# Second attention: the masked corner and the rotary half swap move from TensorE to VectorE

## The reference, cut to what matters

```
def apply_rope(t, cos, sin):
    t1, t2 = jnp.split(tf, 2, axis=-1)
    return jnp.concatenate([t1 * cos - t2 * sin, t1 * sin + t2 * cos], axis=-1)

def mla_attention(q_nope, q_rope, k_nope, k_rope, v):       # 16 heads, 256 positions
    kchunk = jnp.arange(s_len) // CHUNK                      # CHUNK = 64
    ...
        s = (einsum(qn, k_nope) + einsum(qr, k_rope)) * scale      # 128 + 64 wide
        s = jnp.where(kchunk[None, :] <= qchunk[:, None], s, NEG_INF)
        prob = jax.nn.softmax(s, axis=-1)
        return einsum(prob, v)
```

## Time and profile before

| | |
|---|---|
| median of three runs | 2194.48 us |
| the profiled execution's own time | 2193.41 us |
| its span, first to last instruction | 2191.6 us |
| granted TensorE clock | 0.999 |
| PE busy | 2173.5 us (99%) |
| DVE busy | 1385.0 us (63%) |
| ACT busy | 1167.2 us (53%) |
| MLA layer | about 620 to 880 us |

### The profile page before, as it was taken

How to read it: one execution, slowest core, us unless ns; L and a number is a source line. 1 busy time by engine, 2 the same in 40 slices (tenths; PEclk the granted TensorE clock), 3 DMA queues, 4 the chain that set the end, 5 groups by cost and what they waited for, 6 DMA issues and landing times.

```text
span 2191.6 us, 29396 instructions
## 1 busy us (share of the span) xinstructions
PE 2173.5 (99%) x12096; PEld 1872.5 (85%) x12096; DVE 1385.0 (63%) x1750; ACT 1167.2 (53%) x1543; POOL 15.2 (1%) x30
## 2 busy tenths in 40 slices
PE   9999999999999999999999999999999999999998
PEld 8888888888888888888888888888888888888887
DVE  6665555557787666577657788577655544565655
ACT  6555454555766555566545554555444444454443
POOL 1000000000000000000000000000000000000000
PEclk9999999999999999999999999999999999999999
DMA  7555555455646445565655555546566656666655
GB/s 236 177 168 181 184 162 183 154 189 187 188 153 190 138 136 164 180 191 184 201 174 176 158 173 174 193 145 200 173 194 183 200 192 193 183 188 196 200 177 172
DMA packets 223205, 393.98 MB, mean 180 GB/s; under 512 B 20937, under 2 KB 42962, under 8 KB 222944
## 3 DMA queue, kind: packets, MB, share of 16 engines
q1 hardware_dynamic: 221664, 388.35, 56.9%
q0 software_dynamic: 1264, 3.70, 0.5%
q10 hardware_dynamic: 144, 0.07, 0.0%
HBM read 389.96 MB, written 2.11 MB: 179 GB/s over the span
## 4 chain that ended last, share of the span: by engine, by line
PE 80%; DVE 10%; DMA 5%; ACT 3%; issue 1%; DVEq 0%; ACTq 0%
PE ps L896 79%; DVE WL L1440 4%; DMA RAW<-in_w_ple_gate 2%; ACT WH L1165 1%; PE ps L906 1%; DVE T L1440 1%; DMA RAW<-in_w_in 1%; DVE xT L1440 1%; DVE TMP L1440 1%; DMA RAW<-in_w_in_a 1%; DMA RAW<-in_w_gate 1%; DVE H L1443 0%; DVE ACC L1440 0%; DMA RAW<-in_w_up 0%; ACT SQ L1165 0%
## 5 line engine op out<-in xcount | busy, mean ns | idle before, releaser
L1440 DVE TENSOR_TENSOR WL<-RAW,WH 128x1024 fp32r<-128x1024 f32 (+1 forms) x733 | 888.6, 1221 | 474.9 <-ACT WH L1165 471.6
L1165 ACT ACTIVATE WH<-RAW 128x1024 fp32r<-128x1024 f32 (+1 forms) x733 | 770.2, 1056 | 708.9 <-PE ps L896 297.9
L896 PE MATMUL ps<-H,WH 128*128 128x512 f32 x3152 | 1115.2, 398 | 3.2 <-DVE WL L1440 1.3
L896 PE MATMUL ps<-H,WL 128*128 128x256 f32 x3152 | 880.6, 279 | 0.0
L896 PEld LDWEIGHTS ps<-H,WH 128*128 128x128 f32 x3152 | 591.1, 188 | 145.4 <-DVE WL L1440 3.8
L896 PEld LDWEIGHTS ps<-H,WL 128*128 128x128 f32 x3152 | 594.4, 189 | 1.2
L896 PE MATMUL ps<-O,WH 128*128 128x512 f32 (+1 forms) x1376 | 475.8, 393 | 0.2
L896 PE MATMUL ps<-O,WL 128*128 128x256 f32 x1344 | 375.7, 280 | 0.0
L896 PEld LDWEIGHTS ps<-O,WH 128*128 128x128 f32 x1376 | 255.9, 188 | 58.7 <-DVE WL L1440 1.4
L896 PEld LDWEIGHTS ps<-O,WL 128*128 128x128 f32 x1344 | 253.5, 189 | 0.6
L896 PE MATMUL ps<-WH,ACTS 128*128 128x512 f32 x704 | 218.0, 390 | 0.0
(11 more groups left out here) (227 smaller groups left out, 1389.7 us busy)
## 6 DMA issues: line engine op xcount, KB each, us to landing
RAW<-in_w_in_a SPq DMA_DIRECT2D x127, 512.0 KB, 4.0
RAW<-in_w_in SPq DMA_DIRECT2D x96, 512.0 KB, 4.0
RAW<-in_w_gate SPq DMA_DIRECT2D x88, 512.0 KB, 4.1
RAW<-in_w_up SPq DMA_DIRECT2D x88, 512.0 KB, 4.5
RAW<-in_w_down SPq DMA_DIRECT2D x88, 512.0 KB, 4.6
RAW<-in_w_ple_gate SPq DMA_DIRECT2D x64, 512.0 KB, 4.4
RAW<-in_w_in_b SPq DMA_DIRECT2D x40, 512.0 KB, 3.7
RAW<-in_w_out_a SPq DMA_DIRECT2D x32, 512.0 KB, 4.4
```

The source lines that it names most:

```text
L896: return e.matmul(o, l, r, start=start, stop=True, skip_group_check=True)
L1165: return e.activation(o, i, f, **kw)
L1440: return e.tensor_tensor(o, x, y, op)
```

## The change

The permutation matmuls and the step `rope_perm` go, with the constant `perm`. VectorE makes the swap itself: for each group of 32 partitions it multiplies x by sin and writes the result to the partitions 32 away (`r ^ 32`), in four instructions per tile, so eight in place of two for a group j and four in place of one for `kr`. The sin table is stored swapped for this. It now waits for these products before the product with cos. The four `negb[1]` matmuls at the start of `b_scores` go, and the first rotary product starts the bank. In `b_soft` a memset writes -1e30 to the corner, partitions 0 to 63, 4 times 64 columns, and the maxima wait for it. Small tables shrink with it: one 128x128 cast less in `consts`, and one DMA less on POOL's queue.

```
-CONST = ["ident", "tri", "ones", "perm", "mask", "cos", "sin", "negones"]
+CONST = ["ident", "tri", "ones", "mask", "cos", "sin", "negones"]
...
-            pl.bg.append(task(None, do("rope_perm", "kr", bank=[7], frees=[(7, ("ropesin", "kr"))]),
-                              do("rope", "kr", makes=[("rope", "kr")])))
+            pl.bg.append(task(None, do("rope", "kr", makes=[("rope", "kr")])))
...
-                pl.bg.append(task(None, do("rope_perm", j, bank=[7], frees=[(7, ("ropesin", j))]),
-                                  do("rope", j, makes=[("rope", j)])))
+                pl.bg.append(task(None, do("rope", j, makes=[("rope", j)])))
...
-                    for b in (6, 7):
-                        mm(ps[:, b, 0:P], identb[:, :], negb[1][:, :], True)
-                        mm(ps[:, b, S:384], identb[:, :], negb[1][:, :])
-
                     for q0, o in QBLOCKS_B:
                         for j in range(2):
                             r0 = 64 * ((i0 + j) % 2)
                             mm(ps[:, 6 + j, o], qR[s][r0:r0 + 64, (i0 + j) // 2, q0:q0 + P],
-                               KR[r0:r0 + 64, 0:o.stop - o.start])
+                               KR[r0:r0 + 64, 0:o.stop - o.start], o.start == 0)
...
-                elif kind == "rope_perm":
-                    which, war = args
-                    pe.wait_ge(at(*war), at("krs",) if which == "kr" else at("ready", f"rb{which}", 0))
-                    for n_, x in enumerate(rope_tiles(which)):
-                        m = mm(ps[:, 7, n_ * S:(n_ + 1) * S], C["perm"], x, n_ == 0)
-                    m.then_inc(*ev(turned, ("perm", which)))
...
                 elif kind == "b_soft":
                     p, = args
                     dv.wait_ge(at("scores", "B", p))
+                    later = ps[0:64, 6:8, :].rearrange("p b (c x) -> p b c x", c=2)[:, :, :, 64:P]
+                    e.memset(later, -1e30).then_inc(*ev(dve_att))
                     softmax_max(6, 2, 192 ** -0.5, p, "B")
...
-                    dv.wait_ge(at("perm", which), at("in", "cst"), now(x_low))
-                    for n_, x in enumerate(xs):
-                        m = tt(tm[:, n_, :], ps[:, 7, n_ * S:(n_ + 1) * S], C["sin"], ALU.mult)
-                    m.then_inc(*ev(x_low, ("ropesin", which)))
+                    dv.wait_ge(at("krs",) if which == "kr" else at("ready", f"rb{which}", 0), at("in", "cst"), now(x_low))
+                    for r in range(0, P, 32):
+                        for n_, x in enumerate(xs):
+                            m = tt(tm[r ^ 32:(r ^ 32) + 32, n_, :], x[r:r + 32, :], C["sin"][r:r + 32, :], ALU.mult)
+                    m.then_inc(*ev(x_low))
+                    dv.wait_ge(now(x_low))
                     for x in xs:
                         m = tt(x, x, C["cos"], ALU.mult)
                     m.then_inc(*ev(x_low))
...
-    t["sin"] = (np.sin(ang) * np.where(i % 64 < 32, -1.0, 1.0)[:, None]).astype(f)
+    t["sin"] = (np.sin(ang) * np.where(i % 64 < 32, -1.0, 1.0)[:, None]).astype(f)[i ^ 32]
```

More of the change, by code:

```diff
@@ L298, in build @@
         LS = at_("LS", [1, 8], F32, SL[1] + 7200)
-        NG = at_("NG", [P, 2, P], F32, SL[1] + 7232)
+        NG = at_("NG", [P, P], F32, SL[1] + 7232)
         pos[0] = R1 + 69632
@@ L316, in build @@
         identb = sb("identb", [P, P], BF16)
-        negb = [sb(f"negb{i}", [P, P], BF16) for i in range(2)]
+        negb = sb("negb", [P, P], BF16)
         GAIN = sb("GAIN", [P, 256])
@@ L1074, in tensor_engine @@
                         for c in (0, S):
-                            mm(ps[:, b, c:c + P], identb[:, :], negb[0][:, :])
+                            mm(ps[:, b, c:c + P], identb[:, :], negb[:, :])
                         for part in (F1H, F2L):
@@ L1563, in vector_engine @@
                     e.tensor_copy(identb[:, :], C["ident"])
-                    e.tensor_copy(negb[0][:, :], NG[:, 0, :])
+                    e.tensor_copy(negb[:, :], NG[:, :])
                     e.tensor_copy(SUMS[:, 0, :], C["tri"])
-                    e.tensor_copy(SUMS[:, 1, :], C["negones"])
-                    e.tensor_copy(negb[1][:, :], NG[:, 1, :]).then_inc(*ev(small, ("consts",)))
+                    e.tensor_copy(SUMS[:, 1, :], C["negones"]).then_inc(*ev(small, ("consts",)))
                 elif kind == "biasrow":
@@ L1905, in gpsimd_engine @@
                     *ev(landed["cst"], ("in", "cst"), by=16))
-            e.dma_start(NG[:, :, :], cst[:, NCST:NCST + 2 * P].rearrange("p (a b) -> p a b", a=2)).then_inc(
+            e.dma_start(NG[:, :], cst[:, NCST:NCST + P]).then_inc(
                 *ev(landed["neg"], ("in", "neg"), by=16))
@@ L1971, in constants @@
     t["ones"] = np.ones((P, P), f)
-    perm = np.zeros((P, P), f)
-    perm[i ^ 32, i] = 1.0
-    t["perm"] = perm
     t["mask"] = (i[:, None] < i[None, :]).astype(f)
     t["negA"] = np.where(i[:, None] >= i[None, :], f(-1e30), f(0))
-    t["negB"] = np.where((i[:, None] < 64) & (i[None, :] >= 64), f(-1e30), f(0))
     inv = (f(1.0) / (f(10000.0) ** (np.arange(0, 64, 2, dtype=f) / f(64)))).astype(f)
@@ L1980, in constants @@
     t["cos"] = np.cos(ang).astype(f)
-    t["sin"] = (np.sin(ang) * np.where(i % 64 < 32, -1.0, 1.0)[:, None]).astype(f)
+    t["sin"] = (np.sin(ang) * np.where(i % 64 < 32, -1.0, 1.0)[:, None]).astype(f)[i ^ 32]
     t["negones"] = -t["ones"]
-    cst = np.concatenate([t[n].astype(f) for n in CONST + ["negA", "negB"]], axis=1)
+    cst = np.concatenate([t[n].astype(f) for n in CONST + ["negA"]], axis=1)
     d = 255 - np.arange(384)
```

## The result

The changed kernel has a median of 2202.16 us (2199.75 to 2204.48, 6 runs) against 2190.68 us (2187.55 to 2195.91, 6 runs) of the kernel before on the same chip: ratio 1.0050, 95% interval 1.0039 to 1.0062, so 11.0 us more, between 8.5 and 13.6. Timed again beside other kernels it has 2203.89 against 2190.52, ratio 1.0053 (1.0041 to 1.0066). The profiled execution took 2204.48 us, its span is 2202.7 us.

What follows compares the result with a forecast made beforehand. TensorE, busy 99%, was taken as the bound: -6.0 saved + 10.1 waits + 0.4 key + 1.1 memset + 0.2 for pair 3 = +5.8 us, giving 2199.7 us, slower by 0.26%; 8-of-10 range 2192.5 to 2205.5.

Steps and rivals of the forecast that it cites:

- Saved 6.0 us: TensorE, second attention: dropping four groups' permutations saves 3.4 us, dropping eight pairs' corner matmuls 2.6 us.
- The swap, 3.05 us: VectorE, each query group: eight 32-partition products take 3.05 us, between 2.8 and 3.4.
- The waits 3.1, 1.0, 2.9, 3.1 us: TensorE ahead of the scores of groups 0 to 3: waits for VectorE's rotary work, 10.1 us together.
- Rivals 1 and 2: Scores of the four groups: rotary work in time, 2189 us (7%); or waits half as long, 2194 us (17%).
- The memset, 0.27 us, and pairs 0 and 5: Between scores and `b_turn`: memset 0.27 us, 0.35 with hand-over; costs 0.6 at pair 0, 0.35 at pair 5, 1.1 together.
- The key's rotary step, 0.4 us: VectorE, key: the longer step ahead of the second WL delays its chunk on TensorE by 0.4 us (0 to 1).
- rival 3: Four rotary steps: low parts, RAW slots and loads come late, TensorE waits a second time; +10 us, 2204 (8%).
- Rival 4, the clock: Waits before the scores: clock falls to 1.2 GHz in three, losing 2.5 us each; +13 us, 2207 (4%).

Runs made afterwards that it cites:

- mask_only: Kernel before with only the mask moved: memset in place of the corner matmuls, permutations kept on TensorE; 2188.50 us, ratio 0.9988.
- order_n: Changed kernel with the swap's two loops exchanged, so each product has other partitions than the one before it; 2206.26 us, one run.
- after_b: The changed kernel once more, same program, timed beside the version with spare products; 2203.89 us, ratio 1.0053.
- kr_late: Changed kernel with the key's rotary unit moved behind the latent queries' units, query groups as they are; 2203.38 us, ratio 1.0050.
- fill_b: Changed kernel with unused spare matmuls (12, 4, 12, 12) ahead of the scores of pairs 0, 2, 4, 6; 2198.68 us, ratio 1.0034.
- after: The changed kernel as made, against the kernel before; median 2202.16 us, ratio 1.0050, profiled execution 2204.48 us.
- rope_only: Kernel before with only the rotary swap moved to VectorE, corner matmuls kept; 2208.23 us, ratio 1.0078.
- split: Changed kernel with each group's rotary unit done tile by tile, each pair's scores waiting for its own tile; 2192.76 us, ratio 1.0011.
- late1: Changed kernel with one background slot behind each query group's rotary unit, so scores come later; 2191.37 us, ratio 1.0004.
- late2: Changed kernel with two background slots behind each query group's rotary unit, so scores come later; 2190.34 us, ratio 0.9994.
- best2: Changed kernel with two background slots behind each query group's rotary unit and the key's unit behind the latent queries' units; 2188.91 us, ratio 0.9988.

## Why the prediction was right, and where not

The side and the cause were right and the size was short: +5.8 us predicted, 11.0 (8.5 to 13.6) measured, the time in the upper part of the range. That the time itself was only 2.5 us off (2199.7 against 2202.16) is partly luck: the median of three runs that the forecast built on, 2194.48, lies 3.8 us above the median of six that the result is compared with. Step by step:

- **Saved 6.0 us.** Somewhat too much. The corner matmuls were priced at 0.33 us a pair, by their own rows. But the first score matmul behind a chunk now has a start of its own to pay, as the timeline of PE in mask_only shows:

```profile
702.75 0.28 PE L896 MATMUL ps<-CKV,WL 128*128 128x256 f32 x1
702.96 0.93 PE L896 MATMUL ps<-KR,qR 64*128 64x128 f32 x8
```

  From the last WL's start to the scores it is 0.21 us where it was 0.46: 0.25 for this pair, up to 0.41 for others, 2.2 for the eight and not 2.6. The permutation's distance is 3.68 us in the earlier trace rows, not 3.65, which is 0.1 more for the four groups. So 5.7 us saved in all. The balance of the stage: waits grew by 13.6 us, of which 0.6 (the WL at 637.81) only stand where the key's permutation ran; the clock took 7.7, the removed work gave 5.7, together 15.0, and the stage grew by 17.4. The last 2.4 us I can't place. For the mask alone the steps give -2.6 + 0.35 = -2.25, since pair 0 is late only with the moved rotary step; measured -2.5 (interval -5.3 to 0), stage -0.6.
- **The swap, 3.05 us.** Right to the hundredth. The upper bound of 3.4 is the other order of the loops (3.43 in order_n); no run shows the lower one of 2.8.
- **The waits 3.1, 1.0, 2.9, 3.1 us.** Measured 3.07, 1.01, 3.07, 3.08. This is what counting matmuls in the new order against ends in the old VectorE timeline can do. Only group 1, which hangs on a long chain of other work, moved between executions: 1.01 us, 1.76 in after_b, 1.81 in kr_late. Rivals 1 and 2, with these waits absent or halved, fall with it. PE's waits from 690 to 880 us are 12.3 us against a forecast of about 12; in them are 0.7 us for gT at 759.95, ahead of pair 3's scores, where the forecast had 0.2.
- **The memset, 0.27 us, and pairs 0 and 5.** 0.272 us; waits for F of 0.69 and 0.67 against a forecast of 0.6 and 0.63. Right, and PSUM made it no dearer than the two SBUF memsets of the earlier trace rows had suggested.
- **The key's rotary step, 0.4 us.** The term was the direct wait, and that was right (0.32). What was left out is the slot: 0.8 to 2.2 us in place of 0.4. It is rival 3's mechanism, at the one step where the prediction had not looked for it. In the groups it did not come: both waits for WL of the stage, 0.59 and 0.32 us, lie at 637.81 and 643.95, ahead of them.
- **Rival 4, the clock.** This is the term that failed. It was given 4% and the forecast said that the clock stays at 1.00. It fell in three waits of the profiled execution, and its share of the loss is about 5 us by fill_b. The reason for the 4% was the earlier trace rows: behind the last matmul the clock stayed at 1.00 for 5 us. That row was read as a bound, and it isn't one; here the wait began at 701.5, the clock was 1.00 until 705.0 and fell then, when the matmuls already ran again; in the two others it fell at 790.3 and 848.4, some 2 us into the wait. The Trainium skill (TensorE: Matmul & The Clock Gate, section "Why this matters for your kernels") warns against pauses above about 3 us. The waits of 3.07 to 3.44 us agree with that, with a fall at 13 of 15 (after, after_b, rope_only, kr_late, order_n); the falls at a 1.66 and a 1.81 do not, and there the measurement decides. The rival's own price was 2.5 us a wait from 5 us of low clock; measured are 3.4 or 6.8 us of low clock, so up to 1.7 or 3.4 us lost.

With 5 us for the clock, 1 more for the key and 0.3 less saved the sum would have been 12.1 us; measured are 11.5 and 13.4 by the two pairs of medians.

## What to carry to other kernels

Moving work from a full engine to a half idle one pays only where the result's consumer stands far enough behind; count the products that lie between and compare them with the length of the new chain, then move the consumer (three slots here) or hand the result over in halves. Reckon that a long pause of TensorE can cost more than its length: three pauses of 3.1 us cost another 5 us by the clock, three of 1.1 us cost nothing more (split). And a step put ahead of a weight rounding is paid at the load that waits for the slot, 11 us further on.

## What the runs showed of the hardware

- The granted clock can fall after the wait is over, and each low stretch here lasted 3.4 us at 1.2 GHz (ten of them) or 6.8 (five). The totals of a stage are 3.4, 10.2 or 17.1 us in every execution that has a fall. kr_late, behind a wait of 1.81 us (windows, columns as above):

```profile
747.00:748.00 1.00, 1.00 (x7) 0.73 0.06 16
748.00:749.00 1.00, 1.00 (x5) 0.50 0.31 106
749.00:750.00 1.00, 1.00 (x4) 0.50 0.89 260
750.00:751.00 1.00, 1.00 (x5) 0.56 0.41 152
```

- Whether it falls is not set by the length of the wait alone: 3.07 us did it in after and not in after_b at the same place (group 0), 1.66 did and 1.65 did not in one execution. Of eight waits between 1.5 and 2 us it fell behind two (1.66, 1.81) and not behind six: 1.50 in order_n, 1.65 in late1, 1.76 in after_b, 1.82 for F in split, 1.9 for gT in late2 and in best2. Up to 1.1 us no fall was seen. What else decides it, the runs do not show.
- Spare products of 128 columns keep the clock at 1.00 through the same waits, and the kernel that does them is about 5 us faster than the one that idles.
- A memset of 256 float32 columns on 64 partitions of PSUM takes 0.272 us; a product of 256 columns takes 0.42 us on 32 partitions as on 128.
